# Turn of the one-hot and pick of the gates in one product, silu output turned in another bank, gathers spread apart

## The chip, the cores and the metric

The kernel runs on one core of a Trainium2 chip. The metric is the device time of one execution in microseconds, as the median of several runs. The engines are TensorE (PE in the rows, PEld for its weight loads), VectorE (DVE), ScalarE (ACT), GpSimd (POOL) and SyncE (SP), which issues most of the transfers.

## What is computed

The reference is a trunk of two layers over 256 tokens of 1024 float32 values. Each layer has a mixer (attention in chunks, a pooling mixer, differential attention, three gates, an output projection) and then a mixture of experts. Only the experts matter here:

```
x = layer_norm(DN_ALPHA * x + hybrid_mixer(x))
idx, w = route(x)                      # 8 of 64 experts per token, with weights
h = x[tokens of e] @ w_gate_up[e]      # 1024 -> 512, for each expert e
h = silu(h[:, :256]) * h[:, 256:]
y[tokens of e] += (h @ w_down[e]) * gate
x = layer_norm(DN_ALPHA * x + y + shared_expert(x))
```

## The kernel before

The kernel is written engine by engine, and semaphores that are placed by hand set the order. After the mixer and the routing of a layer, the experts are handled in 32 expert steps of two experts each. An expert has 64 slots, so two experts fill 128 rows. Two steps, an even and an odd one, share one gather: four experts, 256 slots. If an expert had more than 64 tokens, more rounds would follow; the profile shows one round in each layer, 64 steps in all.

What a step does, in the order of TensorE's instructions (`pair_step`, line 1302):

- Picks: two products of 4 columns (line 1311) multiply the one-hot matrix of slots by the gate weights, each gate as two parts, and add up over the two halves of the tokens. VectorE sums the parts into `gate_s` (line 1067).
- Turns: two products of 128 columns (line 1314) multiply the same one-hot by the identity, which turns it (transposes it). VectorE copies it to `onehot_t` (line 1083).
- Up: 32 products of 512 columns (line 1326), 64 weight columns each, with the experts' `gu` weights.
- Combine half 0 and half 1: four products each of 512 columns (line 1296), which add the previous step's output `y_hi` and `y_lo` to the accumulators by way of `onehot_t`.
- Between the two halves, two transposes of `hid` (line 1338), after ScalarE's silu (line 690) and VectorE's product with gate and up half (line 1076). VectorE copies them to `hid_t` (line 1079).
- Down: 16 products of 512 columns (line 1351) with the `dn` weights. ScalarE and VectorE split the result into `y_hi` and `y_lo` (lines 699, 1087).

In an odd step the gather for the next two steps is woven in, in four quarters of eight products each (line 1279). Each quarter fills the one bank `bank_gather`, which ScalarE must empty (line 683) before the next quarter begins. Gather 0 stands behind the up product, gathers 1 and 2 behind combine half 1, gather 3 behind the down product. For that VectorE writes a new one-hot (line 913) and copies four gates (line 918) early in the odd step. The last odd step of a layer gathers nothing.

`bank_t` holds three things: the picked gates in columns 0 to 3, then the turned hid in columns 0 to 255, and the turned one-hot in columns 256 to 511. The up product alternates between `bank_even` and `bank_odd`. Its first 256 columns go to silu, the others to line 1076; the second half of the down product is written to the same bank later.

SyncE loads the weights of a step (lines 443 and 447, called from 453 and 457) as soon as the up and the down product that used the buffer are done. Steps 0 to 25 of a layer use three buffers, steps 26 to 31 two.

Of the kernel before, what the change touches and what calls it, by code (L numbers as in the profile page):

```python
# [23 lines left out]
F32R = mybir.dt.float32r  # L24
BF16 = mybir.dt.bfloat16
I32 = mybir.dt.int32
ALU = mybir.AluOpType
ACT = mybir.ActivationFunctionType
AX = mybir.AxisListType.X

P = 128
D = 1024
KD = D // P
S = 256
TT = S // P
# [6 lines left out]
FE = 256  # L42
KF = FE // P
# [77 lines left out]
def build(nc, x, w_in, rel_bias, pool_w, pool_scale, lambda_q1, lambda_k1, lambda_q2, lambda_k2, subln_g,  # L121
# [3 lines left out]
    with ExitStack() as ctx:  # L125
        def sb(name, shape, dt=F32):
            return ctx.enter_context(nc.sbuf_tensor(name, shape, dt))
# [13 lines left out]
        rbias_sb = sb("rbias_sb", [P, L, NE])  # L141
        before_b = sb("before_b", [P, P], BF16)
        ones_b = sb("ones_b", [P, P], BF16)
        ident_r = sb("ident_r", [P, P], F32R)
        gate_s = sb("gate_s", [P, 1])
        eps = sb("eps", [P, 2])
        nlam = sb("nlam", [P, L])
# [16 lines left out]
        slot_of = sb("slot_of", [P, TT, ROUNDS * NE])  # L164
        gate_f = sb("gate_f", [P, TT, NE])
        gate_parts = sb("gate_parts", [P, TT, NE, 2], F32R)
        gate_now = sb("gate_now", [P, TT, 8], F32R)
        onehot = sb("onehot", [P, TT, 2 * P], F32R)
        onehot_t = sb("onehot_t", [P, S], F32R)
        hid = sb("hid", [P, FE])  # L170
        hid_t = sb("hid_t", [P, KF, P])
# [82 lines left out]
        bank_gather, bank_even, bank_odd, bank_t = banks[4:8]  # L254
# [5 lines left out]
        ident = const("ident")  # L260
# [15 lines left out]
        setup_done = sem("setup_done")  # L276
# [26 lines left out]
        gates_ready = sem("gates_ready")  # L303
# [8 lines left out]
        hid_t_ready = sem("hid_t_ready")  # L312
        slots_turned = sem("slots_turned")
        gate_s_ready = sem("gate_s_ready")
        onehot_t_ready = sem("onehot_t_ready")
# [413 lines left out]
        def _(dve):  # L729
# [11 lines left out]
            v = nc.vector  # L741
# [1 line left out]
            dve.wait_ge(const_in, 32)  # L743
            v.tensor_copy(before_b[:], before_in).then_inc(setup_done, 1)
            v.tensor_copy(ones_b[:], const("ones")).then_inc(setup_done, 1)
            v.tensor_copy(ident_r[:], ident).then_inc(setup_done, 1)
            v.memset(eps[:, 0:1], LN_EPS).then_inc(setup_done, 1)
            v.memset(eps[:, 1:2], RMS_EPS).then_inc(setup_done, 1)
            dve.wait_ge(setup_done, 5)
# [165 lines left out]

            def gates(col):

                v.tensor_copy(gate_now[:].rearrange("p t (e a) -> p t e a", e=4),
                              gate_parts[:, :, bass.ds(col, 4), :]).then_inc(gates_ready, 1)

            start = 0
            for l in range(L):
                for task in PLAN:
# [17 lines left out]
                    elif kind == "scores":  # L941
# [6 lines left out]
                        if branch == 0:  # L948
                            if (i, j) == (0, 0):
                                dve.wait_ge(bias_masked, l + 1)  # L950
                            m = 4 * g + j
# [7 lines left out]
                        if j == 1:  # L959
# [5 lines left out]
                            ins = v.reciprocal(recips[:, i % 2, :], sums[:, i % 2, :])  # L965
                            if branch == 1:
                                step(ins)
                                settle()
                                odd = recips[:, i % 2, 1::2]
                                ins = v.tensor_scalar(odd, odd, nlam[:, l:l + 1], None, ALU.mult)  # L970
                            ins.then_inc(recip_ready, 1)
                    elif kind == "pv":
# [3 lines left out]
                        if branch == 0:  # L976
                            dve.wait_ge(y_hi_ready_of[0], 4 * l + i + 1)
                            ins = v.tensor_tensor(y_lo_of[0][where], two, y_hi_of[0][where].bitcast(F32), ALU.subtract)
                        else:
                            wait_task(dve, l, task)  # L980
                            ins = v.tensor_copy(yc_t[where], two)
# [79 lines left out]
                def pair_step(n, odd, combined_before, following=None):  # L1061

                    bank_up, bank_other = (bank_even, bank_odd)[::-1 if odd else 1]
                    dve.wait_ge(slots_turned, n + 1)
                    for e in range(2):
                        rows = slice(SLOTS * e, SLOTS * e + SLOTS)
                        ins = v.tensor_reduce(gate_s[rows, :], bank_t[rows, 2 * e:2 * e + 2], AX, ALU.add)
                    ins.then_inc(gate_s_ready, 1)
                    if following is not None:

                        slots(4 * following)
                        gates(4 * (following & (HALVES - 1)))

                    dve.wait_ge(gate_s_ready, n + 1)
                    dve.wait_ge(silu_ready, n + 1)
                    v.scalar_tensor_tensor(out=hid[:], in0=hid[:], scalar=gate_s[:, 0:1], in1=bank_up[:, FE:2 * FE],  # L1076
                                           op0=ALU.mult, op1=ALU.mult).then_inc(hid_ready, 1)
                    dve.wait_ge(hid_turned, n + 1)
                    v.tensor_copy(hid_t[:], bank_t[:, 0:FE].rearrange("p (k n) -> p k n", k=KF)).then_inc(hid_t_ready, 1)
                    if combined_before is not None:  # L1080

                        dve.wait_ge(combined, combined_before)
                    v.tensor_copy(onehot_t[:], bank_t[:, FE:FE + S]).then_inc(onehot_t_ready, 1)
                    for h in range(2):
                        dve.wait_ge(y_hi_ready, 2 * n + h + 1)
                        part = slice(512 * h, 512 * h + 512)
                        v.tensor_tensor(y_lo[:, part], (bank_other, bank_up)[h][:], y_hi[:, part].bitcast(F32),  # L1087
                                        ALU.subtract).then_inc(y_ready, 1)
# [20 lines left out]
        def _(pe):  # L1109
            mm = nc.tensor.matmul  # L1110
# [12 lines left out]
            for l in range(L):  # L1123
# [144 lines left out]
                def gather(m, q):  # L1268

                    if q == 0:  # L1270
                        pe.wait_ge(s_ready, m + 1)
                    if q:

                        pe.wait_ge(xe_ready, 4 * m + q)
                    for c in range(2):
                        k = 2 * q + c
                        for t in range(TT):
                            for part in (xg_hi, xg_lo):
                                ins = mm(bank_gather[:, 2 * P * c:2 * P * c + 2 * P], part[:, t, k, :], onehot[:, t, :],  # L1279
                                         start=(t == 0 and part is xg_hi), stop=(t == TT - 1 and part is xg_lo))  # L1280
                    ins.then_inc(gathered, 1)
# [20 lines left out]
                def pair_step(n, m, first, odd, slot, loads, last=False):  # L1302

                    bank_up, bank_other = (bank_even, bank_odd)[::-1 if odd else 1]
                    cols = slice(P * odd, P * odd + P)

                    pe.wait_ge(gates_ready, m + 1)
                    if not first:
                        pe.wait_ge(onehot_t_ready, n)
                    for t in range(TT):  # L1310
                        mm(bank_t[:, 0:4], onehot[:, t, cols], gate_now[:, t, 4 * odd:4 * odd + 4],  # L1311
                           start=(t == 0), stop=(t == TT - 1))
                    for t in range(TT):
                        ins = mm(bank_t[:, FE + P * t:FE + P * t + P], onehot[:, t, cols], ident_r[:], start=True, stop=True)  # L1314
                    ins.then_inc(slots_turned, 1)

                    pe.wait_ge(gu_in[slot], (32 if slot == 2 else 16) * loads)
                    if not first:

                        pe.wait_ge(y_ready, 2 * n - 1)  # L1320
                    for k in range(KD):
                        if not odd and k % 2 == 0:

                            pe.wait_ge(xe_ready, 4 * m + k // 2 + 1)
                        for e in range(2):
                            ins = mm(bank_up[SLOTS * e:SLOTS * e + SLOTS, :],  # L1326
                                     xe_t[:, k, P * odd + SLOTS * e:P * odd + SLOTS * e + SLOTS],
                                     gu[slot][:, e, k, :], start=(k == 0), stop=(k == KD - 1))
                    ins.then_inc(up_done, 1)
                    if odd and not last:  # L1330
                        gather(m + 1, 0)
                    if not first:

                        pe.wait_ge(y_ready, 2 * n)
                        combine(0)
                    pe.wait_ge(hid_ready, n + 1)
                    for k in range(KF):
                        ins = nc.tensor.transpose(bank_t[:, P * k:P * k + P], hid[:, k::KF], ident)  # L1338
                    ins.then_inc(hid_turned, 1)
                    if not first:  # L1340
                        combine(1).then_inc(combined, 1)
                    if odd and not last:
                        gather(m + 1, 1)
                        gather(m + 1, 2)
                    pe.wait_ge(hid_t_ready, n + 1)
                    pe.wait_ge(dn_in[slot], 16 * loads)
                    for h in range(2):

                        for k in range(KF):
                            for e in range(2):  # L1350
                                ins = mm((bank_other, bank_up)[h][SLOTS * e:SLOTS * e + SLOTS, :],  # L1351
                                         hid_t[:, k, SLOTS * e:SLOTS * e + SLOTS],
                                         dn[slot][:, e, k, 512 * h:512 * h + 512], start=(k == 0), stop=(k == KF - 1))
                        ins.then_inc(y_done, 1)
                    if odd and not last:
                        gather(m + 1, 3)
# [101 lines left out]
```

## Time and profile before

| | |
|---|---|
| time, median of 3 runs | 1670.34 us (1669.97, 1670.34, 1674.07) |
| the profiled execution | 1673.97 us |
| its span, first to last instruction | 1672.1 us |
| mean granted TensorE clock | 0.975 |
| busy: PE, PEld, DVE, ACT, POOL | 94%, 59%, 32%, 25%, 20% of the span |
| loads from memory | 493.92 MB read, 296 GB/s over the span |

The busy shares are means over the mixer and the expert stage, and the two have different limits. In the expert stages, about 320 to 815 us and again at the end, GpSimd stands still and the transfers run near 400 GB/s. Durations of matmuls in the rows overlap: from one start to the next is the time that a product takes from its successors.

### The profile page before, as it was taken

The numbers are of one execution on the slowest core, as the hardware profiler recorded it, in microseconds if no ns is written. First come the engines' busy times: TensorE is split into PE (matmuls) and PEld (weight loads), VectorE is DVE, ScalarE is ACT, GpSimd is POOL, SyncE is SP. The second block draws the span as 40 slices with busy tenths as digits, with TensorE's granted clock in tenths as the row PEclk, the third lists the DMA queues.
The fourth block names the chain that finished last, engine by engine and source line by source line (L and its number), as shares of the span: only waits on it lengthen the run. The fifth ranks groups of instructions, "written<-read, shape, count | busy, mean of one in ns | idle before, by whom it ended". The sixth has DMA issues, their size and how long they took to land.

```text
span 1672.1 us, 21828 instructions
## 1 busy us (share of the span) xinstructions
PE 1566.4 (94%) x8898; PEld 982.1 (59%) x8898; DVE 532.5 (32%) x914; ACT 413.5 (25%) x653; POOL 331.2 (20%) x94
## 2 busy tenths in 40 slices
PE   4999899999999999999979989989999999999996
PEld 4989895744444444444478889955444444444442
DVE  4246564321222212212232575552212122122223
ACT  2546340111111211211235445221211111111121
POOL 3858570000000000000156676500000000000000
PEclk8999999899999999999979999989999999999998
DMA  8442448599999999779744344586999999995991
GB/s 257 165 146 102 151 153 340 227 428 405 403 376 404 398 381 397 318 314 399 305 139 151 103 150 151 185 369 246 425 389 395 405 398 379 402 398 228 401 402 75
DMA packets 79741, 495.86 MB, mean 297 GB/s; under 512 B 6080, under 2 KB 11456, under 8 KB 46656
## 3 DMA queue, kind: packets, MB, share of 16 engines
q1 hardware_dynamic: 72320, 487.31, 72.5%
q10 hardware_dynamic: 7360, 7.67, 1.5%
q8 instruction: 46, 0.75, 0.2%
q14 instruction: 15, 0.12, 0.0%
HBM read 493.92 MB, written 1.05 MB: 296 GB/s over the span
## 4 chain that ended last, share of the span: by engine, by line
PE 89%; DVE 6%; ACT 2%; ACTq 1%; DMA 0%; issue 0%; POOL 0%; SPq 0%; DVEq 0%
PE bank L1326 27%; PE bank L1167 16%; PE bank L1351 14%; PE bank L1279 8%; PE bank L1296 7%; PE bank L1237 4%; PE bank L1136 3%; PE bank L1254 2%; PE bank L1338 1%; ACT arena L683 1%; PE bank L1314 1%; DVE arena L804 1%; PE bank L1245 1%; PE bank L1287 1%; PE bank L1311 1%; ACT w_hi L574 1%
## 5 line engine op out<-in xcount | busy, mean ns | idle before, releaser
L505 POOL TENSOR_TENSOR w_lo<-ring_w,w_hi 128x2048 fp32r<-128x2048 f32 x64 | 297.2, 4648 | 735.1 <-ACT w_hi L574 722.1
L1167 PE MATMUL bank<-x_hi,w_hi 128*128 128x256 f32 x704 | 207.6, 295 | 21.9 <-DVE x_lo L929 12.7
L1167 PE MATMUL bank<-x_lo,w_hi 128*128 128x256 f32 x704 | 204.0, 290 | 0.0
L1167 PE MATMUL bank<-x_hi,w_lo 128*128 128x256 f32 x704 | 204.0, 290 | 0.0
L1087 DVE TENSOR_TENSOR y_lo<-bank,y_hi 128x512 fp32r<-128x512 f32 x128 | 88.5, 692 | 283.8 <-ACT y_hi L699 283.8
L1326 PE MATMUL bank<-arena 128*64 128x512 f32 x768 | 170.1, 595 | 0.0
L1326 PE MATMUL bank<-gu_a,arena 128*64 128x512 f32 x768 | 170.1, 595 | 0.0
L1076 DVE SCALAR_TENSOR_TENSOR hid<-hid,gate_s,bank 128x256 f32<-128x256 f32 x64 | 30.8, 481 | 414.8 <-ACT hid L690 414.8
L1279 PE MATMUL bank<-onehot,xg_hi 128*128 128x256 f32 x512 | 139.5, 306 | 20.3 <-ACT arena L683 20.3
L1167 PEld LDWEIGHTS bank<-x_hi,w_hi 128*128 128x128 f32 x704 | 140.4, 199 | 26.8 <-issue 23.2
L1279 PEld LDWEIGHTS bank<-onehot,xg_hi 128*128 128x128 f32 x512 | 96.6, 189 | 78.0 <-issue 50.1
L1167 PEld LDWEIGHTS bank<-x_lo,w_hi 128*128 128x128 f32 x704 | 140.3, 199 | 0.2
L1167 PEld LDWEIGHTS bank<-x_hi,w_lo 128*128 128x128 f32 x704 | 140.1, 199 | 0.0
L574 ACT CAST w_hi<-ring_w 128x2048 fp32r<-128x2048 f32 x64 | 121.6, 1902 | 62.5 <-PE bank L1237 44.4
L699 ACT CAST y_hi<-bank 128x512 fp32r<-128x512 f32 x128 | 75.2, 587 | 244.2 <-PE bank L1351 244.2
L690 ACT ACTIVATE hid<-bank 128x256 f32<-128x256 f32 x64 | 24.6, 385 | 447.0 <-PE bank L1326 447.0
L1279 PE MATMUL bank<-onehot,xg_lo 128*128 128x256 f32 x512 | 127.4, 281 | 0.0
L683 ACT COPY arena<-bank 128x512 f32<-128x512 f32 x128 | 75.1, 587 | 179.7 <-PE bank L1279 179.7
L1326 PE MATMUL bank<-ring_w,arena 128*64 128x512 f32 x512 | 113.4, 595 | 0.0
L1296 PE MATMUL bank<-y_hi,onehot_t 128*128 128x512 f32 x256 | 109.6, 428 | 2.8 <-DVE y_lo L1087 2.8
L1326 PEld LDWEIGHTS bank<-gu_a,arena 128*64 128x64 f32 x768 | 52.8, 137 | 97.9 <-issue 96.2
L1326 PEld LDWEIGHTS bank<-arena 128*64 128x64 f32 x768 | 52.7, 137 | 97.9 <-issue 96.2
(181 smaller groups left out, 2148.5 us busy)
## 6 DMA issues: line engine op xcount, KB each, us to landing
gu_a<-in_expert_w_gate_up SPq DMA_DIRECT2D x24, 4096.0 KB, 13.6
arena<-in_expert_w_gate_up SPq DMA_DIRECT2D x24, 4096.0 KB, 13.3
ring_w<-in_expert_w_gate_up SPq DMA_DIRECT2D x32, 2048.0 KB, 8.9
ring_w<-in_w_in SPq DMA_DIRECT2D x25, 2048.0 KB, 8.3
dn_a<-in_expert_w_down SPq DMA_DIRECT2D x24, 2048.0 KB, 11.1
arena<-in_expert_w_down SPq DMA_DIRECT2D x24, 2048.0 KB, 11.0
dn_c<-in_expert_w_down SPq DMA_DIRECT2D x16, 2048.0 KB, 11.4
ring_w<-in_w_out SPq DMA_DIRECT2D x4, 2048.0 KB, 8.3
```

Of the source, the lines that this page charges most:

```text
L505: pool.tensor_tensor(chunk_part(w_lo, n), chunk_in(n), chunk_part(w_hi, n).bitcast(F32), ALU.subtract).then_inc(w_lo_ready, 1)
L574: nc.scalar.copy(chunk_part(w_hi, n), chunk_in(n)).then_inc(w_hi_ready, 1)
L683: nc.scalar.copy(xe_t[:, 2 * q:2 * q + 2, :], bank_gather[:].rearrange("p (c n) -> p c n", c=2)).then_inc(xe_ready, 1)
L699: nc.scalar.copy(y_hi[:, 512 * h:512 * h + 512], (bank_other, bank_up)[h][:]).then_inc(y_hi_ready, 1)
L1087: v.tensor_tensor(y_lo[:, part], (bank_other, bank_up)[h][:], y_hi[:, part].bitcast(F32), ALU.subtract).then_inc(y_ready, 1)
L1136: ins = mm(acc[t][h][:], merged[:, k, P * t:P * t + P], slot_of_block(n, KD)[:, k, :], start=(k == 0), stop=(k == KD - 1))
L1167: ins = mm(b[:, S * c:S * c + S], lhs, rhs, start=(k == 0 and a + w == 0), stop=(k == KD - 1 and a == 1))
L1237: ins = mm(b[:, S * c:S * c + S], w_parts[a][:, k, cols], (y_hi_of, y_lo_of)[w][i][:, k, :], start=(k == 0 and a + w == 0), stop=(k == KW ...
L1279: ins = mm(bank_gather[:, 2 * P * c:2 * P * c + 2 * P], part[:, t, k, :], onehot[:, t, :], start=(t == 0 and part is xg_hi), stop=(t == TT ...
L1296: ins = mm(acc[t][half][:], onehot_t[:, P * t:P * t + P], part[:, 512 * half:512 * half + 512], start=False, stop=True, skip_group_check=True)
L1326: ins = mm(bank_up[SLOTS * e:SLOTS * e + SLOTS, :], xe_t[:, k, P * odd + SLOTS * e:P * odd + SLOTS * e + SLOTS], gu[slot][:, e, k, :], sta ...
L1351: ins = mm((bank_other, bank_up)[h][SLOTS * e:SLOTS * e + SLOTS, :], hid_t[:, k, SLOTS * e:SLOTS * e + SLOTS], dn[slot][:, e, k, 512 * h:5 ...
```

## The change

- The identity and the gates stand side by side in one buffer `turn_pick`: four gate columns for the even step, 128 identity columns, four gate columns for the odd step. One product of 132 columns for each half of the tokens does what the pick and the turn did. The pick is no longer summed over the halves by TensorE; VectorE sums four numbers instead of two. `bank_t` is then two pieces of 132 columns.
- The transposes of `hid` are written to the first 256 columns of the step's own up bank, which silu has read by then.
- In odd steps gather 1 is issued ahead of combine half 1 and gather 2 behind it.
- The gates are copied by two instructions, and the identity is copied twice over at the start.

```diff
-            v.tensor_copy(ident_r[:], ident).then_inc(setup_done, 1)
+            v.tensor_copy(turn_pick[:, :, 4:P + 4], ident.unsqueeze(1).to_broadcast([P, TT, P])).then_inc(setup_done, 1)
...
-                v.tensor_copy(gate_now[:].rearrange("p t (e a) -> p t e a", e=4),
-                              gate_parts[:, :, bass.ds(col, 4), :]).then_inc(gates_ready, 1)
+                for u in range(2):
+                    v.tensor_copy(turn_pick[:, :, (P + 4) * u:(P + 4) * u + 4].rearrange("p t (e a) -> p t e a", e=2),
+                                  gate_parts[:, :, bass.ds(col + 2 * u, 2), :]).then_inc(gates_ready, 1)
...
+                    turned = bank_t[:, 0:TT * (P + 4)].rearrange("p (t n) -> p t n", t=TT)
                     for e in range(2):
                         rows = slice(SLOTS * e, SLOTS * e + SLOTS)
-                        ins = v.tensor_reduce(gate_s[rows, :], bank_t[rows, 2 * e:2 * e + 2], AX, ALU.add)
+                        at_gate = P * odd + 2 * e
+                        ins = v.tensor_reduce(gate_s[rows, :], turned[rows, :, at_gate:at_gate + 2],
+                                              mybir.AxisListType.XY, ALU.add)
...
-                    v.tensor_copy(hid_t[:], bank_t[:, 0:FE].rearrange("p (k n) -> p k n", k=KF)).then_inc(hid_t_ready, 1)
+                    v.tensor_copy(hid_t[:], bank_up[:, 0:FE].rearrange("p (k n) -> p k n", k=KF)).then_inc(hid_t_ready, 1)
...
-                    v.tensor_copy(onehot_t[:], bank_t[:, FE:FE + S]).then_inc(onehot_t_ready, 1)
+                    v.tensor_copy(onehot_t[:].rearrange("p (t n) -> p t n", t=TT),
+                                  turned[:, :, 4 - 4 * odd:P + 4 - 4 * odd]).then_inc(onehot_t_ready, 1)
...
-                    pe.wait_ge(gates_ready, m + 1)
+                    pe.wait_ge(gates_ready, 2 * m + 2)
...
-                        mm(bank_t[:, 0:4], onehot[:, t, cols], gate_now[:, t, 4 * odd:4 * odd + 4],
-                           start=(t == 0), stop=(t == TT - 1))
-                    for t in range(TT):
-                        ins = mm(bank_t[:, FE + P * t:FE + P * t + P], onehot[:, t, cols], ident_r[:], start=True, stop=True)
+                        ins = mm(bank_t[:, (P + 4) * t:(P + 4) * t + P + 4], onehot[:, t, cols],
+                                 turn_pick[:, t, 4 * odd:4 * odd + P + 4], start=True, stop=True)
...
-                        ins = nc.tensor.transpose(bank_t[:, P * k:P * k + P], hid[:, k::KF], ident)
+                        ins = nc.tensor.transpose(bank_up[:, P * k:P * k + P], hid[:, k::KF], ident)
                     ins.then_inc(hid_turned, 1)
+                    if odd and not last:
+                        gather(m + 1, 1)
                     if not first:
                         combine(1).then_inc(combined, 1)
                     if odd and not last:
-                        gather(m + 1, 1)
                         gather(m + 1, 2)
```

TensorE, the start of an even step, behind the down product (L1351, L1354) of the step before or its last gather quarter. Before:

```order
1739 L1279 MATMUL bank<-onehot,xg_hi 128x256
1740 L1279 MATMUL bank<-onehot,xg_lo 128x256
1741 L1311 MATMUL bank<-gate_now,onehot 128x4 x2
1742 L1314 MATMUL bank<-ident_r,onehot 128x128 x2
1743 L1320 ISA
```

Of the change:

```order
1735 L1283 MATMUL bank<-onehot,xg_hi 128x256
1736 L1283 MATMUL bank<-onehot,xg_lo 128x256
1737 L1311 ISA
1738 L1315 MATMUL bank<-turn_pick,onehot 128x132 x2
1739 L1322 ISA
```

Four products have become two of 132 columns.

TensorE, the middle of an odd step, from the transposes of hid to the down product. Before:

```order
1708 L1338 MATMUL bank<-cst,hid 128x128 x2
1709 L1296 MATMUL bank<-y_hi,onehot_t 128x512
...
1712 L1296 MATMUL bank<-y_lo,onehot_t 128x512
1713 L1274 ISA
1714 L1279 MATMUL bank<-onehot,xg_hi 128x256
...
1721 L1279 MATMUL bank<-onehot,xg_lo 128x256
1722 L1274 REGISTER_ALU
1723 L1279 MATMUL bank<-onehot,xg_hi 128x256
...
1730 L1279 MATMUL bank<-onehot,xg_lo 128x256
1731 L1351 MATMUL bank<-dn_a,hid_t 64x512 x8
```

Of the change:

```order
1704 L1340 MATMUL bank<-cst,hid 128x128 x2
1705 L1278 ISA
1706 L1283 MATMUL bank<-onehot,xg_hi 128x256
...
1713 L1283 MATMUL bank<-onehot,xg_lo 128x256
1714 L1300 MATMUL bank<-y_hi,onehot_t 128x512
...
1717 L1300 MATMUL bank<-y_lo,onehot_t 128x512
1718 L1278 REGISTER_ALU
1719 L1283 MATMUL bank<-onehot,xg_hi 128x256
...
1726 L1283 MATMUL bank<-onehot,xg_lo 128x256
1727 L1354 MATMUL bank<-dn_a,hid_t 64x512 x8
```

The wait for ScalarE (L1278 REGISTER_ALU) now has the four combine products ahead of it instead of the gather products themselves, and gather 1's own wait (L1278 ISA) comes right behind the transposes.

## Rows read from the trace of the kernel before

**Rows 1.** The chain that ended last: shares of the span by engine.

```profile
PE 89%; DVE 6%; ACT 2%; ACTq 1%; DMA 0%; issue 0%; POOL 0%; SPq 0%; DVEq 0%
```

**Rows 2.** Who waited for whom, 340 to 1672 us: total us, times, longest us.

```profile
PE bank L1279 <- ACT arena L683: 20.3, 30, 0.7
...
SPq L453 <- PE bank L1326: 448.9, 57, 25.2
SPq L457 <- PE bank L1351: 404.5, 58, 9.2
```

**Rows 3.** Busy time of each engine in stretches, granted clock, DMA share, GB/s.

```profile
core 0: us, PE busy (x) PEld busy (x) DVE busy (x) ACT busy (x) POOL busy (x), PEclk, DMA share, GB/s
280.00:300.00 20.00, 15.45 (x59) 11.08 (x59) 10.79 (x12) 6.55 (x6) 0.00 (x0) 0.75 0.88 352
...
330.00:450.00 120.00, 115.71 (x582) 54.68 (x580) 25.17 (x60) 19.52 (x36) 0.00 (x0) 1.00 0.98 412
...
532.01:550.35 18.34, 17.66 (x97) 9.56 (x95) 4.04 (x10) 3.91 (x7) 0.00 (x0) 1.00 1.01 431
518.42:550.35 31.93, 31.25 (x159) 14.82 (x157) 6.74 (x17) 5.47 (x10) 0.00 (x0) 1.00 0.95 394
```

**Rows 4.** Timeline of an odd step's middle: start us, us, engine, line, operation.

```profile
508.95 0.59 ACT L683 COPY arena<-bank 128x512 f32<-128x512 f32 x1 [0.76 <-PE bank L1279]
...
509.83 0.48 PE L1296 MATMUL bank<-y_hi,onehot_t 128*128 128x512 f32 x1
...
510.85 0.27 PE L1279 MATMUL bank<-onehot,xg_hi 128*128 128x256 f32 x1
...
511.67 0.28 PE L1279 MATMUL bank<-onehot,xg_lo 128*128 128x256 f32 x1
511.99 0.59 ACT L683 COPY arena<-bank 128x512 f32<-128x512 f32 x1 [2.45 <-PE bank L1279]
...
512.62 0.39 PE L1279 MATMUL bank<-onehot,xg_hi 128*128 128x256 f32 x1 [0.68 <-ACT arena L683]
...
512.85 0.28 PE L1279 MATMUL bank<-onehot,xg_lo 128*128 128x256 f32 x1
...
513.77 3.65 PE L1351 MATMUL bank<-dn_c,hid_t 128*64 128x512 f32 x16
```

**Rows 5.** Timeline, TensorE and its weight loads at the start of an even step.

```profile
518.30 0.31 PEld L1311 LDWEIGHTS bank<-gate_now,onehot 128*128 128x128 f32 x2
518.42 0.28 PE L1311 MATMUL bank<-gate_now,onehot 128*128 128x4 f32 x2
518.53 0.30 PEld L1314 LDWEIGHTS bank<-ident_r,onehot 128*128 128x128 f32 x2
518.56 0.42 PE L1314 MATMUL bank<-ident_r,onehot 128*128 128x128 f32 x2
...
518.91 7.09 PE L1326 MATMUL bank<-gu_a,arena 128*64 128x512 f32 x32
```

**Rows 6.** Timeline, TensorE at the start of an odd step.

```profile
532.01 0.38 PE L1311 MATMUL bank<-gate_now,onehot 128*128 128x4 f32 x2
532.26 0.42 PE L1314 MATMUL bank<-ident_r,onehot 128*128 128x128 f32 x2
532.61 0.65 PE L1326 MATMUL bank<-arena 128*64 128x512 f32 x2
```

**Rows 7.** Timeline, VectorE in an odd step: the gate copy and what follows.

```profile
502.39 0.17 DVE L918 CAST gate_now<-gate_parts 128x16 fp32r x1
...
508.30 0.48 DVE L1076 SCALAR_TENSOR_TENSOR hid<-hid,gate_s,bank 128x256 f32<-128x256 f32 x1 [5.74 <-ACT hid L690]
```

**Rows 8.** A 4096 KB load's time to landing; issue and use with two buffers.

```profile
gu_a<-in_expert_w_gate_up SPq DMA_DIRECT2D x24, 4096.0 KB, 13.6
...
718.01 0.39 SPq L443 DMA_DIRECT2D gu_a<-in_expert_w_gate_up  x1
...
742.44 7.09 PE L1326 MATMUL bank<-gu_a,arena 128*64 128x512 f32 x32
```

**Rows 9.** Timeline, VectorE at the start of the kernel.

```profile
16.77 0.21 DVE L746 CAST ident_r<-cst 128x128 fp32r<-128x128 f32 x1
```

More of the change, by code:

```diff
@@ L143, in build @@
         ones_b = sb("ones_b", [P, P], BF16)
-        ident_r = sb("ident_r", [P, P], F32R)
         gate_s = sb("gate_s", [P, 1])
@@ L166, in build @@
         gate_parts = sb("gate_parts", [P, TT, NE, 2], F32R)
-        gate_now = sb("gate_now", [P, TT, 8], F32R)
+        turn_pick = sb("turn_pick", [P, TT, P + 8], F32R)
         onehot = sb("onehot", [P, TT, 2 * P], F32R)
```

## The prediction

> **What bounds the kernel now.** I read the chain of waits first, then who waited for whom, the windows of the expert stage, and last the timeline of one pair of expert steps. The chain that ends last lies on TensorE for 89% of the span [rows 1], so time is won by taking work or idle time from TensorE. In the list of waits its largest wait is for ScalarE at line 1279: 20.3 us in 30 waits, none above 0.7 us [rows 2]. No wait of TensorE for a transfer stands in the expert stage; it is the other way round, since SyncE waits for TensorE's products before it issues each load (448.9 and 404.5 us) [rows 2]. An even and an odd step together take 31.93 us, and TensorE runs at its upper level, 2.4 GHz (granted clock 1.00), with 31.25 us of it busy; the DMA engines are already busy 0.95 of that time, moving 394 GB/s [rows 3]. There are 16 such pairs of steps in a layer, so about 2 x 511 us of the 1672.1 us lie here, and the change touches nothing else but one copy at the start.
>
> **Part 1, gathers spread apart (odd steps only).** Today combine half 1 (four products, 509.83 to 510.85) stands ahead of gather 1, and gather 2 right behind it. Gather 2 needs the bank that ScalarE still has to empty: the last product of gather 1 starts at 511.67, the copy runs from 511.99 to 512.58, gather 2 starts at 512.62 [rows 4]. Products of a gather otherwise follow one another after 0.12 us, so 0.95 - 0.12 = 0.83 us is lost, and the restart costs more: the second product follows the first after 0.23 us instead of 0.12 [rows 4]. Together 0.94 us. After the change combine half 1 stands between the two. It lasts 1.02 us, and from gather 1's last product to gather 2's first there are then some 1.06 to 1.14 us, against the 0.95 that ScalarE needs: the wait is covered with only 0.1 to 0.2 us to spare. Gather 1 in turn moves up to where combine half 1 began, 509.83. It needs the copy of gather 0, which ran 508.95 to 509.54 [rows 4], so 0.25 us are to spare there. I take off 0.03 us, since the slow first product behind the transposes now falls on a gather instead of a combine: 0.91 us a step. With 30 such waits [rows 2] (the last odd step of each layer gathers nothing) that is 27.3 us. Bounds: if only the 0.68 us of idle time at 512.62 goes and gather 1 pays a restart of 0.11, 17 us; if all goes, 28 us.
>
> What is queued behind: on VectorE the turned one-hot's copy waits for combine half 1, which ends about 0.9 us later, and ahead of the y differences that start only after the down product (513.77 [rows 4] at the earliest). I cost it at nothing. Should that cover go, the next step's first product would wait for it. The copy to hid_t stands ahead of it on VectorE and is not held back.
>
> **Part 2, one product instead of two.** An even step starts its picks at 518.42, its turns at 518.56, its up product at 518.91: 0.49 us. [rows 5] An odd step takes 532.01 to 532.61, 0.60 us, because the pipeline restarts there [rows 6]. The turns alone take 0.35 us up to the up product in both. Four columns more on 128 are 3%, so I give the pair of 132 columns 0.36 us behind a gather, and 0.45 us behind the down product, where the first of the pair carries the restart (0.23 as in the gathers). Saved: 0.13 us in an even and 0.15 us in an odd step, 0.14 x 64 steps = 9.0 us. Bound above: the two weight loads that go are 0.115 us each (518.30 to 518.53 for the picks' two [rows 5]), so 0.23 us a step, 15 us. Bound below, a loss: if 132 columns ran at the pace of the combine's 512, 1.02 us for four [rows 4], the pair would take about 0.51 us and 0.1 us more to hand over to the up product: 0.1 us slower per step, 6 us. I stay with 9, because the 128-column row is by far the nearest.
>
> The trace spaces those two loads at 0.115 us [rows 5], and that spacing, not the columns, seems to set the pace of small products. The Trainium skill ("TensorE: Matmul & The Clock Gate", LDWEIGHTS) agrees: it gives a load as its columns over 1.2 GHz, 107 ns for 128. By that rule alone two loads less save 0.21 us a step, 14 us instead of 9.
>
> **Part 3, the rest.** Silu output turned into its up product's bank: the same two transposes and the same copy, in another bank; the transposes already wait for hid, behind silu. Nothing. The gate copy becomes two, 0.17 us each by the old one, and each gate sum reads four elements instead of two; VectorE sits idle 5.74 us behind them until silu is there, which hides it [rows 7]. Without that cover they would cost 0.2 us in 32 steps, 6 us. At the start the identity is copied twice over, and that copy took 0.21 us in the chain ahead of x_lo [rows 9]: 0.1 us more, lost in rounding.
>
> **Sum.** 27.3 + 9.0 - 0.1 = 36 us. The profiled execution took 1673.97 us (span 1672.1), which gives 1638. It lies 3.6 us above the median of the runs, 1670.34, whose other two runs lie within 0.4 us of each other. A median of the changed kernel is compared with that median, so I forecast 1670.3 - 36 = **1634 us**.
>
> **What is late next.** A pair of steps becomes 31.93 - 0.91 - 0.28 = 30.74 us and asks for the same 12.58 MB (31.93 us at 394 GB/s [rows 3]), now 409 GB/s. The row with the engines fully busy shows 431 GB/s, and 120 us at the head of the stage ran at 412 [rows 3]: a floor of 29.2 to 30.5 us a pair. A load of 4096 KB lands after 13.6 us; in the stretch with two buffers it is issued at 718.01 and used at 742.44, 10.8 us to spare [rows 8]. With three buffers it is half a pair more, about 27 us. The transfers therefore come near, and TensorE still ends last.
>
> **Rivals.**
> - *Weight loads set the pace* (the rule above as this kernel's mechanism): part 2 gives 15 us, time 1628. For it speaks the even 0.115 us; against it the 0.35 us of the turns, which two loads do not fill. 0.14.
> - *Gather 2 still waits*: the spare 0.1 us is gone because combine half 1 without its slow first product is shorter, or ScalarE comes later. Half of part 1 stays, 22 us won, time 1648. 0.10.
> - *The wide product is slow* as in part 2's lower bound: 27 - 6 = 21 us won, 1649. 0.04.
> - *Transfers hold the two-buffer stretch*: were a pair of loads no faster than 31.93 us, 13 pairs with three buffers would eat 13 x 1.19 = 15 us of 27 to spare and cost nothing, and the last three pairs of each layer would win nothing: 2 x 3 x 1.19 = 7 us less, 1641. 0.06.
> - *Nothing comes of it*: gather 1 meets at its new place, and the wide product at its own, what they were to escape; 1670. Against it stands the 0.25 us to spare. 0.03.
> - *Slower, by transfers*: asked for more, the DMA engines give less, and TensorE waits at the up product. With a pair of loads lasting P, a layer's stage takes 16 P - 27 us. It passes today's 511 us when P exceeds 33.6 us, below 374 GB/s. At 370 GB/s it is 517 us, so 1682. Waits long enough would also bring the granted clock down, as where TensorE was busy 15.45 of 20 us and the clock was 0.75 [rows 3]. The 412 GB/s speak against it. 0.03. The Trainium skill ("HBM Reference", Specifications) gives a core 358 GB/s as its share and about 425 when it streams alone. By 358 the stage would take 535 us and the kernel 1718; the trace already runs above that and fits the second figure.
>
> **How the numbers follow.** The forecast has 0.60. Its own range is 1627 to 1647: 43 us won with both parts at their upper bound, 23 us with part 1 at its lower bound of 17 and each wide product dearer by 0.02 us than I gave it (a loss in part 2 is the third rival). Taking in 1628, 1641 and part of 1648 and 1649 gives 1624 to 1649, with less than 2 in 10 outside. A measurement of this kernel tells about 0.3% (5 us) from no change. All cases but the last two are faster by more than that: 0.94. Same 0.03, slower 0.03.
>
> **What would show it.** Right: no wait for ScalarE left at the gathers' line (now 20.3 us); an odd step of 17.3 us instead of 18.34, an even step of 13.46 instead of 13.59 from first product to first product; from the product of 132 columns to the up product 0.36 and 0.45 us; DMA share near 0.98 in a pair. Wrong: a wait at gather 1 or 2 of more than 0.1 us, 132 columns lasting near 400 ns, or any wait of TensorE for gu or dn in the stage.

## The result and the profile after

The changed kernel took 1628.94 us (median of 4 runs, 1627.95 to 1629.77) against 1670.15 us before (4 runs): a ratio of 0.9746, interval 0.973 to 0.9761. It is faster by 41 us; forecast were 36 us less and 1634 us, with a range of 1624 to 1649. The profiled execution took 1627.95 us, its span 1626.2.

The windows of the changed kernel, cut again at the first product of an even step, of the odd step behind it, and of the next even one (columns as in [rows 3]):

```profile
core 0: us, PE busy (x) PEld busy (x) DVE busy (x) ACT busy (x) POOL busy (x), PEclk, DMA share, GB/s
478.26:491.63 13.37, 13.37 (x63) 5.05 (x61) 2.71 (x7) 1.56 (x3) 0.00 (x0) 1.00 0.99 402
491.63:508.78 17.15, 17.15 (x94) 9.17 (x93) 4.09 (x11) 3.90 (x7) 0.00 (x0) 1.00 1.01 429
478.26:508.78 30.52, 30.52 (x154) 14.21 (x153) 6.80 (x18) 5.46 (x10) 0.00 (x0) 1.00 1.00 417
```

A pair of steps went from 31.93 us [rows 3] to 30.52, and TensorE has no idle time left in it. The even step gained 0.22 us (13.59 to 13.37), the odd one 1.19 us (18.34 to 17.15). The list of waits of TensorE in the changed kernel, longest first, begins with two waits of the mixer and one of the last combines of a layer, all three as long as before (total us, times, longest us):

```profile
PE bank L1153 <- DVE x_tok L791: 11.9, 3, 4.6
PE bank L1241 <- DVE arena L981: 7.4, 1, 7.4
PE bank L1300 <- DVE y_lo L1091: 2.8, 2, 1.4
```

The wait for ScalarE that led it, 20.3 us in 30 times [rows 2], is gone. The middle of an odd step, the changed kernel's timeline, answers to [rows 4]:

```profile
501.15 0.36 PE L1283 MATMUL bank<-onehot,xg_hi 128*128 128x256 f32 x1
...
502.06 0.28 PE L1283 MATMUL bank<-onehot,xg_lo 128*128 128x256 f32 x1
...
502.18 0.39 PE L1300 MATMUL bank<-y_hi,onehot_t 128*128 128x512 f32 x1
...
502.38 0.59 ACT L682 COPY arena<-bank 128x512 f32<-128x512 f32 x1 [1.52 <-PE bank L1283]
...
503.02 0.19 PEld L1283 LDWEIGHTS bank<-onehot,xg_hi 128*128 128x128 f32 x1 [0.18 <-ACT arena L682]
503.11 0.30 PE L1283 MATMUL bank<-onehot,xg_hi 128*128 128x256 f32 x1
...
504.16 3.65 PE L1354 MATMUL bank<-dn_c,hid_t 128*64 128x512 f32 x16
```

From gather 1's last product to gather 2's first there are 1.05 us, the combine between them taking 0.93. ScalarE's copy ends at 502.97, 0.91 us behind gather 1's last start as before [rows 4], and gather 2's weight load, which has waited 0.18 us for it, follows at 503.02. The product starts at 503.11, 0.24 us behind the last combine product, which is the combine's own pace. So ScalarE still holds up the load but no longer the product, and about 0.1 us of cover is left. The next product follows after 0.13 us, where it was 0.23 [rows 4].

The starts of an even and an odd step answer to [rows 5] and [rows 6]:

```profile
478.14 0.30 PEld L1315 LDWEIGHTS bank<-turn_pick,onehot 128*128 128x128 f32 x2
478.26 0.34 PE L1315 MATMUL bank<-turn_pick,onehot 128*128 128x132 f32 x2
...
478.52 0.20 PEld L1328 LDWEIGHTS bank<-arena 128*64 128x64 f32 x4
478.52 7.09 PE L1328 MATMUL bank<-arena 128*64 128x512 f32 x32
...
491.63 0.44 PE L1315 MATMUL bank<-turn_pick,onehot 128*128 128x132 f32 x2
...
492.00 7.09 PE L1328 MATMUL bank<-ring_w,arena 128*64 128x512 f32 x32
```

From first product to up product it is now 0.26 us in the even step (0.49 before) and 0.37 us in the odd one (0.60 before): 0.23 us saved in each, where I had 0.13 and 0.15.

Steps add up to the result: 30 pairs x 1.41 us + 2 pairs without a gather x 0.46 us = 43 us, against 41 us of the medians. The traces repeat such steps to some hundredths of a microsecond, while medians of the same kernel differ by up to 3.6 us from one set of runs to another, so below both are given.

### The profile page after: what moved, and what is told of

Same layout as the page of the kernel before. It is cut to its first block, busy times and chain, and to the rows that moved or that the text cites. A ratio compares the mean times of both kernels' runs of the same rounds, so it can differ in the third digit from the quotient of the medians.

```text
span 1626.2 us, 21647 instructions
## 1 busy us (share of the span) xinstructions
PE 1540.6 (95%) x8770; PEld 960.6 (59%) x8770; DVE 517.1 (32%) x946; ACT 413.4 (25%) x653; POOL 332.8 (20%) x94
## 3 DMA queue, kind: packets, MB, share of 16 engines
HBM read 493.92 MB, written 1.05 MB: 304 GB/s over the span
## 4 chain that ended last, share of the span: by engine, by line
PE 90%; DVE 6%; ACT 1%; ACTq 1%; DMA 0%; issue 0%; POOL 0%; SPq 0%; DVEq 0%
PE bank L1328 28%; PE bank L1171 17%; PE bank L1354 14%; PE bank L1283 8%; PE bank L1300 8%; PE bank L1241 4%; PE bank L1140 3%; PE bank L1258 2%; PE bank L1340 1%; PE bank L1315 1%; DVE arena L803 1%; PE bank L1249 1%; PE bank L1291 1%; ACT w_hi L573 1%; PE bank L1183 1%; DVE arena L804 1%
## 6 DMA issues: line engine op xcount, KB each, us to landing
gu_a<-in_expert_w_gate_up SPq DMA_DIRECT2D x24, 4096.0 KB, 14.1
```

## The experiments

All times are medians. The runs came in sets, each with the kernel before on the same chip; its medians lay between 1669.9 and 1673.5 us and its lowest times between 1668.3 and 1669.2, so a difference between sets is uncertain by some 1 to 3 us. Open were whether the two edits act by themselves, whether the new bank has a price, what sets the price of a small product, and how near the transfers are.

### One edit at a time

The single product alone is the changed kernel with this edit undone:

```diff
-                    if odd and not last:
-                        gather(m + 1, 1)
                     if not first:
                         combine(1).then_inc(combined, 1)
                     if odd and not last:
+                        gather(m + 1, 1)
                         gather(m + 1, 2)
```

> The change with its gathers put back in the old place, so that the single product of 132 columns acts alone. Theory A, each small product costs its weight load and two loads of 0.11 us go per step: 0.22 x 64 = 14 us less than before, about 1656 us; first product to up product 0.26 us in an even step, 0.37 in an odd one. Theory B, my sum's 0.14 us per step: 9 us less, 1661.

Measured: 1656.02 us against 1671.3, ratio 0.9907 (0.9891 to 0.9923), 15.3 us less. The wait that the other edit removes stands in its profile as before:

```profile
PE bank L1283 <- ACT arena L682: 20.3, 30, 0.7
```

Theory A holds; 1661 is outside the interval's 1653 to 1658. The trace is sharper. From the first up product of a layer to that of its 32nd step, 31 steps later, the kernel before takes 492.3 us and this one 485.4: 0.224 us less per step, 0.112 for each load that went. From first product to up product it shows 0.27 and 0.37 us, as Theory A said.

The gathers alone is the reverse edit in the kernel before.

> The kernel before with gather 1 ahead of combine half 1 and nothing else. Both theories: the 30 waits of 0.68 us and their restarts go, 0.93 to 0.96 us each, 28 us less than before, about 1642 us. If part of the gain of 41 us was an interplay of the two edits, this and the single product alone add up to clearly less than 41.

Measured: 1642.77 us, ratio 0.9826 (0.9811 to 0.9842), 28.5 us less, 0.95 us for each of 30 gathers. By the trace, 31 steps take 478.1 us instead of 492.3, again 0.95 us for each of the 15 gathers of a layer. Its timeline shows gather 1's last and gather 2's first product 1.05 us apart, as in the changed kernel:

```profile
506.28 0.28 PE L1279 MATMUL bank<-onehot,xg_lo 128*128 128x256 f32 x1
...
507.33 0.30 PE L1279 MATMUL bank<-onehot,xg_hi 128*128 128x256 f32 x1
```

The hid bank alone is two words in the kernel before:

```diff
-                        ins = nc.tensor.transpose(bank_t[:, P * k:P * k + P], hid[:, k::KF], ident)
+                        ins = nc.tensor.transpose(bank_up[:, P * k:P * k + P], hid[:, k::KF], ident)
...
-                    v.tensor_copy(hid_t[:], bank_t[:, 0:FE].rearrange("p (k n) -> p k n", k=KF)).then_inc(hid_t_ready, 1)
+                    v.tensor_copy(hid_t[:], bank_up[:, 0:FE].rearrange("p (k n) -> p k n", k=KF)).then_inc(hid_t_ready, 1)
```

> The kernel before with the transposes of hid written to the up product's own bank and nothing else. My theory: no difference, 1670 us. Rival: the other bank has a price or a gain of its own (a write ordered behind the reads of silu and of line 1076), seen as more than 5 us either way.

Measured: 1670.53 us, ratio 0.9998 (0.9986 to 1.0009), and 31 steps take 492.3 us as before. No price.

> The changed kernel itself, unaltered, timed once more. If the two edits only add up, it lies 15.3 + 28.5 = 43.8 us under the kernel before; if they share a part of their gain, at the 41 us of the first measurement or less.

Measured: 1627.47 us against 1669.89, 42.4 us less (ratio 0.9729, 0.9708 to 0.975). The two edits alone give 43.8. The 1.4 us between them are less than the intervals of each. The traces settle it: 31 steps of the changed kernel take 471.1 us, 21.2 less than before, and the two edits alone take off 6.9 and 14.3. They add up.

### What a small product costs

Four kernels add two products per step ahead of the pair of 132 columns, and a fifth does so with half the weights. Their output is overwritten at once:

```diff
                     for t in range(TT):
+                        mm(bank_t[:, 0:P], onehot[:, t, cols], turn_pick[:, t, 4:P + 4], start=True, stop=True)
+                    for t in range(TT):
                         ins = mm(bank_t[:, (P + 4) * t:(P + 4) * t + P + 4], onehot[:, t, cols],
```

For 4 columns the moving operand is `turn_pick[:, t, 0:4]`, for 256 and 512 `xg_hi[:, t, 0:2, :]` and `xg_hi[:, t, 0:4, :]`; for half the weights it is `onehot[:, t, P * odd:P * odd + SLOTS]` with 128 columns.

> The changed kernel with two more products of 128 columns per step ahead of the pair of 132, written to a bank that the pair then overwrites. Theory A (weight load, 0.115 us each): 0.23 x 64 = 15 us more than the changed kernel, about 1644. Theory B (the 0.35 us that I read for two products of 128 columns): 22 us more, 1651.

> The changed kernel with two more products of 4 columns per step, same weights. Theory A (weight load): the same price as two of 128 columns, 15 us more than the changed kernel, 1644. [...]

> The changed kernel with two more products of 256 columns per step. Theory A: the columns take 0.107 us at 2.4 GHz, just under the load's 0.115, so again 15 us more, 1644. Theory B: 2 x (0.35 us) or more, over 1651.

> The changed kernel with two more products of 512 columns per step. Both theories: now the columns set the pace, 0.235 us each as in the combine, 0.47 x 64 = 30 us more, 1659; a check that the added products do cost what their rows say.

> The changed kernel with two more products of 128 columns per step whose weights are 64 columns instead of 128. Theory A (the load sets the pace, by its columns): half the price of the 128-column load or a little over, 0.06 us each, 8 us more, 1637. Rival (each instruction of TensorE costs the same, whatever it loads): 15 us more, 1644. A change of the weights' shape may cost a hand-over of its own of some 0.1 us, which would add 6 us to either.

The changed kernel measured 1628.94 and 1627.47, so I count from 1628.2; there are 128 added products. The last two columns are from the traces: the 31 steps of a layer, 471.1 us in the changed kernel, and what they took more, shared among the 62 products added to them.

| weights x columns | us | more | per product | 31 steps | per product |
|---|---|---|---|---|---|
| 128 x 4 | 1641.72 | 13.5 | 0.106 | 478.2 | 0.114 |
| 128 x 128 | 1641.58 | 13.4 | 0.105 | 478.2 | 0.114 |
| 128 x 256 | 1642.98 | 14.8 | 0.115 | 478.5 | 0.119 |
| 128 x 512 | 1659.34 | 31.1 | 0.243 | 485.8 | 0.236 |
| 64 x 128 | 1636.76 | 8.6 | 0.067 | 475.7 | 0.074 |

Up to 256 columns the price hardly depends on the columns (had they set it, two products of 4 columns would have cost next to nothing), and with half the weights it falls. So it is neither the columns nor a fixed price of an instruction: the weight load sets it. At 512 columns the columns take over. The Trainium skill ("TensorE: Matmul & The Clock Gate", LDWEIGHTS) gives a load as the columns of the weights over 1.2 GHz, 107 ns for 128 and 53 ns for 64. These runs show somewhat more, by the traces 114 ns for 128 and 74 for 64. The 74 are a mean. In odd steps, behind the down product with its 64 weight columns, the start of the step grew by 0.12 us for the two products, 60 ns each; in even steps, behind the gather's 128, by 0.18 us, 88 ns each. So some 0.06 us of an even step may be a hand-over of the changed shape, which no run tries alone.

The start of an even step, in the timelines of the kernels with added products of 4 and of 512 columns and with 64 weights:

```profile
480.44 0.28 PE L1315 MATMUL bank<-turn_pick,onehot 128*128 128x4 f32 x2
480.58 0.42 PE L1317 MATMUL bank<-turn_pick,onehot 128*128 128x132 f32 x2
480.93 7.09 PE L1330 MATMUL bank<-arena 128*64 128x512 f32 x32
```

```profile
482.71 0.63 PE L1315 MATMUL bank<-xg_hi,onehot 128*128 128x512 f32 x2
483.18 0.33 PE L1317 MATMUL bank<-turn_pick,onehot 128*128 128x132 f32 x2
483.44 7.09 PE L1330 MATMUL bank<-arena 128*64 128x512 f32 x32
```

```profile
481.05 0.29 PE L1315 MATMUL bank<-turn_pick,onehot 128*64 128x128 f32 x2
481.17 0.39 PE L1317 MATMUL bank<-turn_pick,onehot 128*128 128x132 f32 x2
481.49 7.09 PE L1330 MATMUL bank<-arena 128*64 128x512 f32 x32
```

Look at the pair of 132 columns: behind two products of 4 columns it seems to take 0.35 us up to the up product, behind 512 columns 0.26, and alone 0.26. The first number is the one that I read for the turns in the kernel before. The difference lies in where the pair's first product starts. Behind the 4-column products it starts 0.03 us after its own weight load (480.56 and 480.58 in that trace), since the loads follow one another every 0.11 us and nothing else holds it up; behind 512 columns its load comes 0.24 us ahead of it, in the shadow of the product before (482.94 and 483.18).

### How near the transfers are

Three kernels leave out part of the up product (one, two and four of eight parts of the inner dimension), so that TensorE has less to do and the loads stay. Here for one part:

```diff
+                        if k >= 7:
+                            continue
                         for e in range(2):
...
-                                     gu[slot][:, e, k, :], start=(k == 0), stop=(k == KD - 1))
+                                     gu[slot][:, e, k, :], start=(k == 0), stop=(k == 7 - 1))
```

> The changed kernel with the last of eight parts of the inner dimension left out of the up product: each step issues 28 instead of 32 of its products, 0.86 us less, and the loads stay as they are. If TensorE alone sets the stage, 0.86 x 64 = 55 us less, about 1574 us, and a pair of steps takes 28.8 us. If the transfers are the next bound at the 431 GB/s that the busiest row of before showed, a pair cannot fall under 29.2 us where the buffers give no slack.

> The changed kernel with two of the eight parts of the inner dimension left out of the up product, 1.72 us less per step. TensorE alone: 110 us less, 1519, a pair 27.1 us. Transfers at 431 GB/s: a layer's stage is at least 16 x 29.2 - 27 = 440 us instead of TensorE's 434, so 1531, with waits of TensorE for gu or dn in the second half of the stage.

> The changed kernel with four of the eight parts left out of the up product, 3.44 us less per step. TensorE alone would give 220 us less, 1409. Transfers at 431 GB/s hold a layer's stage at 440 us or above: some 1530 us again. The pair of steps in the middle of the stage then shows the floor of the transfers by itself.

Measured: 1573.73, 1560.17 and 1558.44 us. The first eighth pays in full: 54.5 us of 55 expected, and a pair of steps takes 28.8 us in its trace. The second gives 13.6 us instead of 55, the next two 1.7 us together. The windows 450 to 570 us of the three kernels, in this order:

```profile
450.00:570.00 120.00, 120.00 (x600) 56.19 (x598) 29.29 (x73) 23.02 (x42) 0.00 (x0) 1.00 1.01 426
```

```profile
450.00:570.00 120.00, 118.07 (x602) 58.33 (x600) 28.70 (x72) 24.55 (x45) 0.00 (x0) 1.00 1.01 426
```

```profile
450.00:570.00 120.00, 104.14 (x488) 50.05 (x486) 27.28 (x69) 22.41 (x41) 0.00 (x0) 0.91 1.01 426
```

All three move 426 GB/s with the DMA engines fully busy; that is the ceiling here over such a stretch (single steps show 429 and 431), and it makes 12.58 MB in 29.5 us. In the last, TensorE idles and its mean granted clock falls to 0.91. The time does not rise with it (1558.44 us), so a clock that falls while TensorE waits for transfers costs nothing visible here. The waits for transfers, absent with one eighth less, are these with two eighths less:

```profile
PE bank L1330 <- DMA arena<-in_expert_w_gate_up: 20.9, 10, 2.8
...
PE bank L1330 <- DMA ring_w<-in_expert_w_gate_up: 8.5, 4, 2.4
```

and with four eighths less:

```profile
PE bank L1330 <- DMA arena<-in_expert_w_gate_up: 43.3, 14, 4.2
...
PE bank L1330 <- DMA ring_w<-in_expert_w_gate_up: 26.9, 8, 4.1
PE bank L1330 <- DMA gu_a<-in_expert_w_gate_up: 26.3, 6, 4.5
```

The kind of bound was as expected, but 1530 us was not: these kernels end at 1558 to 1560. By the stage's length: the changed kernel's 16 x 30.52 = 488 us a layer shrank by half of 68 us, to 454, and 16 x 29.5 is 472. The buffers thus give 18 us of slack in a layer, not the 27 that I had. Where the other 9 us go no run tries, but the trace with two eighths less points to the first loads of the stage. Its first up product starts at 326.47 us, and the third buffer's up weights are issued in two halves 11 us apart, the second only when the stage begins; the down weights follow at 327.61:

```profile
315.56 11.17 SPq L442 DMA_DIRECT2D ring_w<-in_expert_w_gate_up  x2
```

So at least 4.2 of its 6.3 MB are missing at the start, 9.8 us at 426 GB/s (an estimate). The time to landing of the 4096 KB loads is no such limit by itself. As a median it was 13.6 us before [rows 8], is 14.1 in the changed kernel, and 19.8 with one eighth less, where TensorE still never waits for a load; the rows of the changed kernel and of that one:

```profile
gu_a<-in_expert_w_gate_up SPq DMA_DIRECT2D x24, 4096.0 KB, 14.1
```

```profile
gu_a<-in_expert_w_gate_up SPq DMA_DIRECT2D x24, 4096.0 KB, 19.8
```

No kernel here that does the full work beats the changed one.

## Why the prediction was right, and where it was off

- **What bounds the kernel**: right. TensorE sets the stage; one part of the up product less gives its full 54.5 us.
- **Part 1, the gathers**: right in mechanism and nearly in size. Forecast 0.91 us per odd step, measured 0.95 (the gathers alone, 28.5 us in 30) and 0.96 (the odd step's 1.19 less 0.23). Of the cover of 0.1 to 0.2 us that I gave, the lower end came (1.05 us against the 0.95 that ScalarE needs), since the combine took 0.93 us in its new place instead of 1.02. Gather 2's product is not held up, though its load is.
- **Part 2, one product instead of two**: right in direction, too small. Forecast 9 us, measured 15.3 alone. The step that failed is "The turns alone take 0.35 us up to the up product in both", from which I gave the new pair 0.36 and 0.45 us; it takes 0.26 and 0.37. The 0.35 us was no property of two products of 128 columns. Read from load to load, the pair takes the same in both kernels: 0.38 us from its first load to the up product (518.53 to 518.91 [rows 5], now 478.14 to 478.52), of which 0.26 lie between its second load and the up product's first. The second load and the up product's first, before and then after:

```profile
518.64 0.19 PEld L1314 LDWEIGHTS bank<-ident_r,onehot 128*128 128x128 f32 x1
518.90 0.14 PEld L1326 LDWEIGHTS bank<-gu_a,arena 128*64 128x64 f32 x2
```

```profile
478.26 0.19 PEld L1315 LDWEIGHTS bank<-turn_pick,onehot 128*128 128x128 f32 x1
478.52 0.14 PEld L1328 LDWEIGHTS bank<-arena 128*64 128x64 f32 x2
```

The loads' own rows had the answer. Four of them lay between 518.30 and the up product before [rows 5], two do now, each worth 0.11 us. The upper bound of 0.23 us per step was the true value, and the rival by which weight loads set the pace (1628 us, chance 0.14) was the case that came. "Against it the 0.35 us of the turns, which two loads do not fill" was a misreading: one spacing of two loads and the 0.26 us behind the last one make 0.38, and the first turn starts 0.03 us into them. The 0.26 us are the same in the full-work kernels here, in all 64 steps; what they consist of, no run tries.
- **Part 3**: right. The new bank costs nothing (ratio 0.9998). That the gate copies cost nothing was not tried alone, but the single product alone contains them, and its steps gained the two loads in full. The two take 0.24 us together and VectorE still idles 5.45 us behind them, in the changed kernel's timeline:

```profile
493.94 0.24 DVE L918 CAST turn_pick<-gate_parts 128x8 fp32r x2
...
499.62 0.48 DVE L1079 SCALAR_TENSOR_TENSOR hid<-hid,gate_s,bank 128x256 f32<-128x256 f32 x1 [5.45 <-ACT hid L689]
```

- **The sum**: forecast 36 us, the steps of the trace give 43, the medians 41.2 and 42.4. By the runs of each part alone, part 2 brought 6.3 us more than forecast and part 1 1.2 us more. The total came near because part 1 was three quarters of the sum; part 2 was worth 1.7 times its forecast.
- **Transfers**: near, and not the bound, as I had it. The DMA share rose to 1.00 in the pair shown and 0.99 over the middle of the stage, where I had 0.98; the pair became shorter than forecast. A pair of steps stands 1.0 us above the 29.5 us of the transfers. In the stretch with two buffers, which I held to be the tighter one, the share falls to 0.86 and TensorE stays fully busy. The changed kernel's windows (columns as in [rows 3]):

```profile
450.00:570.00 120.00, 120.00 (x600) 56.09 (x596) 26.70 (x66) 21.25 (x39) 0.00 (x0) 1.00 0.99 413
...
640.00:760.00 120.00, 120.00 (x602) 55.63 (x600) 26.67 (x67) 21.45 (x39) 0.00 (x0) 1.00 0.86 360
```

- **The slower rival** needed the transfers to give less when asked for more, below 374 GB/s. They gave more, 417 in the changed kernel's pair and 426 over 120 us where more was asked. The Trainium skill ("HBM Reference", Specifications) has about 425 GB/s for a core alone, and that is what these runs show.

## What to carry to other kernels

At the full granted clock, a small product on TensorE with 128 weight columns costs its weight load (0.11 us here), whatever its columns up to some 256: joining two products that share their weights is worth one load, and widening one is nearly free. Read its price from the spacing of the loads' rows and not from a product's start to its successor, since a product can start right with its load or well behind it. Before taking out more work, take some out on purpose and see when the time stops following; here that came between 54 and 68 us below the changed kernel.

## What the runs showed of the hardware that I had not expected

- A product of 4 columns costs as much as one of 128 (0.114 us each by the traces), and one of 256 only 0.005 us more.
- Between the last weight load of 128 columns and the first load of the up product, whose shape differs, 0.26 us pass, in all 64 steps of every kernel here that does the full work.
- A kernel whose DMA engines are already busy 0.99 of the time in the middle of a stage (413 GB/s) still let TensorE win another 54.5 us before it waited for a transfer at all. The ceiling was 426 GB/s over 120 us, the buffers held the rest, and a load's time to landing could grow from 14.1 to 19.8 us unseen.
